# A recurrence's next-head projection issued from five places of a head's steps in place of ten

## What is computed

```
dec  = exp(where(mask, bcum_t - bcum_s, -inf))          # bcum: running sum of log f
att  = einsum('bthk,btshk,bshk->bhts', q, dec, k)
o    = att @ v + (q * exp(bcum)) @ S
S    = exp(bcum_last) * S + (k * exp(bcum_last - bcum))^T @ v
```

## Time and profile before

| | |
|---|---|
| median of 3 runs | 1960.88 us (1958.27 to 1968.60) |
| profiled execution, its own time | 1963.67 us |
| its span, first to last instruction | 1961.8 us |
| mean granted clock of TensorE | 0.982 |
| TensorE busy | 1853.4 us, 94% |
| VectorE busy | 817.3 us, 42% |
| ScalarE busy | 597.5 us, 30% |
| GpSimd busy | 457.8 us, 23% |

### The profile page before, as it was taken

The page is one execution under the profiler, slowest core; times in us unless marked ns, Lnnn a source line. Parts: engine busy times, 40 slices in busy tenths (PEclk is TensorE's granted clock), DMA queues, the critical chain, the costliest instruction groups (busy, mean ns, idle before and its releaser), DMA issues. The chain is left out here.

```text
span 1961.8 us, 31675 instructions
## 1 busy us (share of the span) xinstructions
PE 1853.4 (94%) x13519; PEld 1513.4 (77%) x13519; DVE 817.3 (42%) x1523; ACT 597.5 (30%) x1174; POOL 457.8 (23%) x363
## 2 busy tenths in 40 slices
PE   5998999989999789999999999999989999999998
PEld 4644455659999446666678998999889999999986
DVE  5225466571100344445422545565552115551333
ACT  3211333442111433223302444434342223222311
POOL 0000011001220125455107600000015544454300
PEclk8999999999999889999999999999999999999999
DMA  9304000021110436845114722222143334433322
GB/s 313 160 0 165 6 12 12 1 92 43 44 44 22 155 112 223 324 153 167 50 38 102 210 64 53 53 53 53 45 117 86 82 96 142 120 85 93 108 75 86
DMA packets 193223, 189.32 MB, mean 97 GB/s; under 512 B 48285, under 2 KB 156381, under 8 KB 192957
## 3 DMA queue, kind: packets, MB, share of 16 engines
q1 hardware_dynamic: 169932, 134.13, 22.6%
q0 software_dynamic: 20592, 52.63, 9.1%
q10 hardware_dynamic: 2560, 0.56, 0.2%
HBM read 162.65 MB, written 31.92 MB: 99 GB/s over the span
## 5 line engine op out<-in xcount | busy, mean ns | idle before, releaser
L348 DVE TENSOR_SCALAR sb<-sb 128x1024 int32<-128x1024 int32 (+4 forms) x145 | 101.7, 706 | 372.4 <-DMA sb<-in_w_in 148.7
L2765 POOL TENSOR_TENSOR weights_low<-sb 128x1536 fp32r<-128x1536 f32 x42 | 148.0, 3523 | 175.9 <-DVE sb L348 175.9
L2888 PE MATMUL ps<-h_high_again,weights_high 128*128 128x272 f32 x688 | 142.3, 288 | 2.0 <-ACT weights_high L2804 2.0
L2888 PE MATMUL ps<-h_low,weights_high 128*128 128x272 f32 x688 | 142.3, 288 | 0.0
L2888 PE MATMUL ps<-h_high_again,weights_low 128*128 128x272 f32 x688 | 142.3, 288 | 0.0
L2888 PEld LDWEIGHTS ps<-h_high_again,weights_high 128*128 128x128 f32 x688 | 108.2, 188 | 2.2 <-ACT weights_high L2804 2.2
L2888 PEld LDWEIGHTS ps<-h_high_again,weights_low 128*128 128x128 f32 x688 | 108.4, 188 | 0.0
L2888 PEld LDWEIGHTS ps<-h_low,weights_high 128*128 128x128 f32 x688 | 108.3, 188 | 0.0
L2234 PE MATMUL ps<-h_high_again,recurrence_weights_high 128*128 128x384 f32 (+1 forms) x432 | 104.1, 349 | 2.2 <-ACT sb L2050 1.2
L689 POOL TENSOR_TENSOR sb<-sb 32x1088 f32<-32x1088 f32 x8 | 19.9, 2484 | 367.1 <-ACT sb L700 367.1
L1098 POOL DMA_INDIRECT sb<-in_cache_kv_latent,sb x64 | 60.6, 947 | 158.9 <-PE ps L1665 76.1
(11 more groups left out here) (347 smaller groups left out, 4047.0 us busy)
## 6 DMA issues: line engine op xcount, KB each, us to landing
sb<-in_w_in SPq DMA_DIRECT2D x82, 512.0 KB, 4.2
sb<-in_w_branch SPq DMA_DIRECT2D x48, 256.0 KB, 4.5
sb<-in_x_prompt SPq DMA_DIRECT2D x16, 512.0 KB, 4.8
values_by_level<-values POOLq DMA_DIRECT2D x56, 128.0 KB, 4.5
sb<-values_by_level POOLq DMA_DIRECT2D x7, 896.0 KB, 7.7
out<-sb SPq DMA_DIRECT2D x10, 512.0 KB, 2.8
h_low_in_dram<-h_low_staged SPq DMA_DIRECT2D x8, 544.0 KB, 3.6
h_high_in_dram<-h_high_staged SPq DMA_DIRECT2D x8, 544.0 KB, 4.3
```

The source lines that it names most:

```text
L348: return nc.vector.tensor_scalar(high.bitcast(I32), x.bitcast(I32), -4096, None, ALU.bitwise_and)
L2765: nc.gpsimd.tensor_tensor(flat(wLowR[slot]), flat(wLow[slot]), flat(wHigh[slot]), ALU.subtract)\
L2888: mm = nc.tensor.matmul(bank(4 * (k % 2) + s, n=HS2), w[:, c, :], x[:, t0:t0 + HS2], start=c == 0 and part == 0, stop=c == DC - 1 and part ...
```

## The change

One line: the table of the steps 1 to 7. The table of step 8, the order of the head's own work and every other engine's code stay as they are.

```
-            AFTER = {"l0": 2, "l1": 2, "l2": 2, "l3": 2, "l4": 1, "l5": 1, "l6": 1, "l7": 1, "turn": 1, "states": 3}
+            AFTER = {"l0": 4, "l2": 4, "l5": 2, "turn": 2, "states": 4}
             LAST = {"l0": 2, "l1": 2, "l2": 2, "l3": 2, "l4": 1, "l5": 1, "l6": 0, "l7": 0, "turn": 1, "states": 1,
                     "output": 2, "sums": 2}
             assert sum(AFTER.values()) == sum(LAST.values()) == 2 * DC
```

## The result

The changed kernel takes 2010.09 us (median of 4 runs, 2007.48 to 2014.57) against 1961.70 before (4 runs, 1958.27 to 1968.60): 1.0246 times, with an interval of 1.0216 to 1.0277. The forecast was 1991, its range ended at 2006. The change costs 48.4 us, 18 more than forecast. The profiled execution after took 2007.48 us, with a span of 2005.6 and a mean granted clock of 0.976.

What follows compares the result with a forecast made beforehand. TensorE alone was taken to bound steps 1 to 7. Waits less switch gains, 4 x 5.05 + 3 x 2.75 = 28.45 us, plus 1.5 for the clock, took the median of 1960.88 to 1991 us, range 1979 to 2006.

Steps and rivals of the forecast that it cites:

- The clock: Granted clock in the recurrence: one more fall to half clock than before, 1.5 us added to the forecast.
- Switches: TensorE, steps 1 to 7: ten places become five, each place costing 0.19 us, so 0.95 us saved a step.
- Level 1: Behind level 1, TensorE waits 1.69 us ahead of level 2 in steps 1, 2, 4, 6; 0 in steps 3, 5, 7.
- Level 3: Behind level 3, no wait ahead of level 4's work; in steps 3, 5, 7 a wait of 0.28 us for `spread_roots`.
- Level 4: Behind level 4, TensorE waits ahead of level 5: 2.11 us in steps 1, 2, 4, 6; 1.64 in 3, 5, 7.
- Level 6: Behind level 6, no wait ahead of level 7 in steps 1, 2, 4, 6; up to 0.05 us in the others.
- Level 7: Behind level 7, TensorE waits 2.20 us ahead of the turning in all seven steps, a price read from step 8.
- Steps without the clock: Step lengths from waits and switches: step 4 at about 48.3 us, step 3 at 50.4.
- The signs: Trace of the changed kernel: waits ahead of levels 2, 5 and the turning; TensorE busy 1 us less in steps 3 and 4.
- the last sign of being wrong: The prediction is wrong if the granted clock in the recurrence lies clearly under 0.97.
- The second rival: The clock falls at most waits: 13 falls of 1.54 us, 20.0 us on top of 28.45, 2009 us; chance 0.13.

Runs made afterwards that it cites:

- the waits kept busy: Changed kernel plus six calls (12 unread matmuls) behind levels 4 and 7, and behind level 1 in steps without norm sums: 1989.19 us against 1961.14 (1.0149).
- the second traces of both kernels: The kernel before and the changed kernel each profiled once more, nothing altered: 13 falls in steps 1 to 7 after, none before; step 8 before took 54.11 us.
- the first run with busy waits: Changed kernel plus twelve calls (24 unread matmuls) behind levels 4 and 7 of steps 1 to 7, level 1 left bare: 2005.2 us against 1959.15 (1.022).

## Why the prediction was wrong

The step that failed is the one headed "The clock": "From that I take one more fall than before, 1.5 us". There are 13 falls in the steps 1 to 7, and the price of one was right: 1.54 in the forecast, 1.44 and 1.58 in the stretches above. Between the second traces of both kernels the steps 1 to 7 grow from 315.6 us (1379.37 - 1063.81) to 364.4 (1427.73 - 1063.31), by 48.9. With the waits kept busy they take 344.8 (1407.39 - 1062.62), so 29.2 are the waits and switches (forecast 28.45) and 19.6 are the clock: 13 x 1.51.

By its own steps:

- *Switches.* A fill of four parts was 6.14 us against 6.15. In the steps the gain is a little less than 0.19 a place: step 4 with the part behind level 7 put back is busy for 42.53 us, four places fewer than 43.20, so 0.17 a place. The place behind level 7 taken away alone gave nothing (43.19 against 43.20).
- *Level 1*: 1.65 against 1.69, in four steps, none in the three with norm sums. Right.
- *Level 3*: none, and 0.45 against 0.28 ahead of `spread_roots`. Undersized by 0.5 us in all.
- *Level 4*: 2.05 against 2.11, and 1.53 against 1.64. Right, with the sigmoid ahead of gather 5 as the cause: putting parts there only moved the wait to the sigmoid itself in the four steps without norm sums.
- *Level 6*: none. *Level 7*: 2.12 against 2.20. Right.
- *Steps without the clock*: 48.15 and 50.68 measured with busy waits, 48.25 and 50.37 forecast.
- *The signs.* The waits were there and the steps 3 and 4 did not grow alike, but the last sign of being wrong came true: the granted clock is 0.93 or 0.94 in six of the seven steps. TensorE's busy time in step 4 did not fall by 1 us but rose by 2.2.
- *The clock.* The second rival was the true case in its mechanism, and 2009 us for 2010.09 measured. That its count was met is partly luck: it had seven falls behind level 7, four behind level 4 and two behind norm sums, and there are seven, six and none. It had a chance of 0.13, and the range stopped below it.

What misled was one row. Over step 8's two waits the clock stood at 1.00 in the earlier trace rows, and I took it as evidence that waits of this length keep the clock. It was one execution of one place, and the exception of ten: the second trace of before has a fall at the same waits. Against it stood the fall of step 7 behind norm sums, without any wait.

The Trainium skill's "TensorE: Matmul & The Clock Gate" ("HAM oscillation — how this bites in real kernels") tells of a kernel that starts cold behind every wait for its transfers. The waits in that section of the Trainium skill are longer than the 18 here, so it doesn't forecast falls for this change, as the prediction took it to. The trace goes further: 13 of the changed kernel's 18 waits of 1.5 to 2.2 us are followed by a fall.

Left open is which waits are followed by a fall. Of 24 waits of 1.65 us behind level 1, in six traces that hold them bare, one was (step 4 of the first run with busy waits); 2.12 ahead of the turning were in seven of seven and, with other places covered, in four of seven; 2.05 and 1.53 ahead of level 5 in six of seven and in two of seven. Length alone does not order these. Nor does what a step holds: with the part back behind level 7, step 2 has a fall behind level 5's wait and step 4 has none, with the same work and the same waits. Neither the instants at which the waits come nor the work beside them was varied by itself.

## What to carry to other kernels

When work that fills holes on the bounding engine is moved, price each bare place by the chain across the other engines, row by row: that gave 29 us to within 1. Then price the clock separately, as a case with a range of its own: many waits of about two microseconds among small matmuls cost here two thirds as much again as the waits themselves, and one clean place in one trace is no evidence that it will hold. If TensorE must wait, matmuls that nobody reads, shorter than the wait, can be worth more than idleness.

## What the runs showed that I had not expected

- Adding 12 unused matmuls in each of 18 waits took the changed kernel from 2010 to 1989 us; 24 of them at 14 places, longer than the waits, still left step 2 faster than idle ones, 49.43 against 51.19 us.
- A fall does not hang on its own wait alone: covering the wait ahead of the turning took falls away from the untouched waits ahead of level 5 (six to two), and the other way round (seven to four). These are single traces, and the instants of the waits moved too, so that the other wait is the cause is not shown.
- A call with 128 x 128 operands of this type makes two matmuls: six calls show as twelve in the trace, 1.60 us.
